# Mixture-of-experts stage on Trainium2: prompt rows picked by one-hot products ahead of the first expert, sample rows turned in pairs of blocks

## What is computed

```python
def ec_moe(h, w_router, w_gate, w_up, w_down):
    xf = h.reshape(N, D)
    aff = jax.nn.softmax((xf @ w_router).astype(jnp.float32), axis=-1)
    cap = CAPACITY_FACTOR * N // N_EXPERTS
    gates, idx = lax.top_k(aff.T, cap)
    xe = xf[idx]
    hid = jax.nn.silu(jnp.einsum('ecd,edf->ecf', xe, w_gate)) * jnp.einsum('ecd,edf->ecf', xe, w_up)
    ye = jnp.einsum('ecf,efd->ecd', hid, w_down) * gates[..., None].astype(h.dtype)
    out = jnp.zeros((N, D), h.dtype).at[idx.reshape(-1)].add(ye.reshape(-1, D))
```

## Time and profile before

| | us |
|---|---|
| median of 3 runs | 3549.77 (3549.66 to 3550.65) |
| the profiled execution's own time | 3553.03 |
| its span | 3551.3 |
| mean granted TensorE clock over the span | 0.968 |
| PE busy | 3315.4 (93%), 23082 matmuls |
| DVE busy | 2314.5 (65%) |
| ACT busy | 1628.7 (46%) |
| POOL busy | 638.6 (18%) |
| mean DMA rate | 153 GB/s |

### The profile page before, as it was taken

The page is one execution under the profiler, slowest core; times in us unless marked ns, Lnnn a source line. Parts: engine busy times, 40 slices in busy tenths (PEclk is TensorE's granted clock), DMA queues, the critical chain, the costliest instruction groups (busy, mean ns, idle before and its releaser), DMA issues. The chain is left out here.

```text
span 3551.3 us, 68456 instructions
## 1 busy us (share of the span) xinstructions
PE 3315.4 (93%) x23082; PEld 3024.3 (85%) x23082; DVE 2314.5 (65%) x3871; ACT 1628.7 (46%) x3584; POOL 638.6 (18%) x866
## 2 busy tenths in 40 slices
PE   7978999999999999999997992999999999999997
PEld 3877998998998998996665882999999999999997
DVE  3877887887887887886774446555555555555553
ACT  2435665665665665664442111433434334444332
POOL 0542222222222223221000000010100100000001
PEclk8999999999999999999998995999999999999998
DMA  6644434434434434433225542555666565555553
GB/s 222 219 178 140 128 114 153 127 114 153 127 114 153 127 114 134 129 114 105 95 67 208 194 183 83 178 176 178 181 187 188 185 185 179 179 178 178 179 179 85
DMA packets 357239, 542.43 MB, mean 153 GB/s; under 512 B 26104, under 2 KB 280568, under 8 KB 341882
## 3 DMA queue, kind: packets, MB, share of 16 engines
q1 hardware_dynamic: 346880, 505.26, 43.3%
q0 software_dynamic: 10240, 35.66, 4.6%
HBM read 439.11 MB, written 101.74 MB: 152 GB/s over the span
## 5 line engine op out<-in xcount | busy, mean ns | idle before, releaser
L2140 PE MATMUL ps_gu<-xT,e_w 128*128 128x272 f32 x6144 | 789.3, 290 | 5.8 <-DVE xT L2287 5.6
L2140 PEld LDWEIGHTS ps_gu<-xT,e_w 128*128 128x128 f32 x6144 | 779.6, 189 | 9.6 <-issue 9.3
L2282 DVE TENSOR_TENSOR e_w<-e_raw,e_w 128x2048 fp32r<-128x2048 f32 x192 | 440.0, 2292 | 341.8 <-ACT e_w L2207 325.5
L913 ACT ACTIVATE e<-ps_s,negm 128x1024 f32<-128x1024 f32 (+1 forms) x384 | 465.9, 1218 | 229.0 <-DVE negm L1195 229.0
L1187 DVE TENSOR_REDUCE mx<-ps_s 128x1 f32<-128x1024 f32 (+2 forms) x396 | 519.7, 1319 | 78.3 <-PE ps_s L642 78.3
L642 PE MATMUL ps_s<-kT,qT 128*128 128x512 f32 (+1 forms) x1920 | 473.8, 387 | 28.3 <-ACT e L913 16.8
L678 PE MATMUL ps_m<-v,aT 128*128 128x128 f32 x3456 | 477.2, 280 | 2.9
L678 PEld LDWEIGHTS ps_m<-v,aT 128*128 128x128 f32 x3456 | 424.1, 192 | 31.9 <-issue 16.1
L642 PEld LDWEIGHTS ps_s<-kT,qT 128*128 128x128 f32 x1920 | 351.8, 193 | 95.2 <-ACT e L913 16.5
L2159 PE MATMUL ps_gu<-hid,e_w 128*128 128x272 f32 x3072 | 417.6, 292 | 0.0
L712 PE MATMUL ps_m<-w,hT 128*128 128x384 f32 x2040 | 393.1, 341 | 3.4 <-DVE o L1242 1.8
(11 more groups left out here) (261 smaller groups left out, 3530.0 us busy)
## 6 DMA issues: line engine op xcount, KB each, us to landing
hT<-hT_d SPq DMA_DIRECT2D x85, 1024.0 KB, 5.6
e_raw<-w_gate SPq DMA_DIRECT2D x64, 1024.0 KB, 5.2
e_raw<-w_up SPq DMA_DIRECT2D x64, 1024.0 KB, 5.3
e_raw<-w_down SPq DMA_DIRECT2D x64, 1024.0 KB, 7.4
qT_d<-qT_out SPq DMA_DIRECT2D x96, 256.0 KB, 5.7
qT<-qT_d SPq DMA_DIRECT2D x96, 256.0 KB, 2.8
tab<-tabs_d SPq DMA_DIRECT2D x85, 256.0 KB, 2.7
hT_d<-hT SPq DMA_DIRECT2D x17, 1024.0 KB, 4.0
```

Source lines behind the costliest of these rows:

```text
L913: nc.scalar.activation(out, src, ACT.Exp, bias=negm[:, s.par, c:c + 1], scale=HD ** -0.5, accum_out=acc).then_inc(exp_done.sem, 1)
L2140: mm = nc.tensor.matmul(ps_gu[:, 2 * (s % 2) + f, 0:SLOTS], w_view(s, a)[:, k, f * P:f * P + P], xT[:, b, k, :], start=(k == 0 and a + b = ...
L2282: nc.vector.tensor_tensor(w[:, s % RING, 1, :], raw[:, s % RAW, :], w[:, s % RING, 0, :].bitcast(F32), ALU.subtract).then_inc(w_lo, 1)
```

## The change

The 16 prompt rows no longer go through the gather and the turns. The prompt's 128 rows of h2 are loaded once (`h2p`), a one-hot table of all 16 experts is made (`hot_all`), and 8 products of 256 columns (`pick`) yield the turned prompt rows of all experts, which ACT and DVE split into `xTp`. For each expert ACT then copies 256 elements per partition from `xTp` into `xT` (`place_prompt`). The sample rows are turned in four steps of four transposes, one step for each down slab. In a down slab the step and `turn_back(e, d - 1)` now both stand between the two halves. The diff, where lines are left out for length they are names, semaphores and the unchanged one-hot of expert e:

```diff
@@ -1994,7 +1994,11 @@
         g_cur = sb("g_cur", [P, 3])
         i_next = sb("i_next", [P, 3], U32)
         i_cur = sb("i_cur", [P, 3], U32)
-        xg = sb("xg", [P, 3, D])
+        xg = sb("xg", [P, 2, D])
+        h2p = sb("h2_prompt", [P, D])
+        hot_all = sb("hot_all", [P, NE, CAPP])
+        xTp = sb("xT_prompt", [P, NE, 2, KD, CAPP], F32R)
         xT = sb("xT", [P, 2, KD, SLOTS], F32R)
         sg_ = sb("silu_g", [P, 2, SLOTS])
         h32 = sb("e_h32", [P, 2, SLOTS])
...
-            return ps_gu[:, k % 4, :] if isinstance(e, int) and e == 0 else ps_x[:]
+        PAIRS = KD // 2
+        def turned_at(e, p):
+            bank = ps_gu[:, p, :] if isinstance(e, int) and e == 0 else ps_x[:]
+            return bank.rearrange("p (k c) -> p k c", k=2)
+        def picked_at(p):
+            return ps_d[:, p % 3, :].rearrange("p (k e c) -> p k e c", k=2, e=NE)
         def run_experts(eng, body):
...
@@ -2038,6 +2050,7 @@
         @block.sync
         def _(sp):
+            sp.dma_start(h2p[:], g.h2[NS * P:NT * P, :]).then_inc(h2p_in, 16)
             sp.dma_start(gate2[:, 0, :], g.mod[0, 5 * D:6 * D].partition_broadcast(P)).then_inc(gate2_in, 16)
             sp.dma_start(gate2[:, 1, :], g.mod[1, 5 * D:6 * D].partition_broadcast(P)).then_inc(gate2_in, 16)
@@ -2064,11 +2077,10 @@
             def gather(e):
                 hold(idx_done, e + 1)
-                hold(xT_ready, KD * e)
-                for n in range(3):
-                    rows = CAPP if n == 0 else P
-                    nc.gpsimd.indirect_dma_start(xg[0:rows, n, :], None, g.h2,
-                                                 bass.IndirectOffsetOnAxis(i_next[0:rows, n:n + 1], 0)
+                hold(xT_ready, PAIRS * e)
+                for n in range(2):
+                    nc.gpsimd.indirect_dma_start(xg[:, n, :], None, g.h2,
+                                                 bass.IndirectOffsetOnAxis(i_next[:, n + 1:n + 2], 0)
                                                  ).then_inc(gathered, 16)
             def scatter(e):
@@ -2095,24 +2107,37 @@
         def _(pe):
             def make_list(e):
                 wait_positive(pe, hot_done, 3 * e + 3)
-                wait_positive(pe, xT_lo, KD * e)
+                wait_positive(pe, xT_lo, PAIRS * e)
                 for half in range(2):
                     for t in range(NS):
                         nc.tensor.matmul(ps_x[:, 5 + 5 * half:10 + 5 * half], hot[:, t, half * P:half * P + P],
                                          vcur[:, t, :], start=(t == 0), stop=(t == NS - 1))
                 nc.tensor.matmul(ps_x[0:CAPP, 0:5], hot_p[:], vcur[:, NS, :], start=True, stop=True).then_inc(listed, 1)
-            def turn(e, k):
-                if k == 0:
-                    wait_positive(pe, gathered, 48 * e + 48)
+            def pick(p):
+                if p == 0:
+                    pe.wait_ge(h2p_in, 16)
+                    pe.wait_ge(hot_all_done, 1)
+                if p >= 3:
+                    pe.wait_ge(xTp_lo, p - 2)
+                for m in range(2):
+                    at = (2 * p + m) * P
+                    mm = nc.tensor.matmul(picked_at(p)[:, m], h2p[:, at:at + P], hot_all[:], start=True, stop=True)
+                mm.then_inc(xTp_ready, 1)
+            def turn(e, p):
+                if p == 0:
+                    wait_positive(pe, gathered, 32 * e + 32)
                     wait_positive(pe, found_done, 2 * e + 2)
-                bank = turned_at(e, k)
-                wait_positive(pe, xT_lo, k - 3 if isinstance(e, int) and e == 0 else KD * e + k)
-                for n in range(2):
-                    nc.tensor.transpose(bank[:, CAPP + n * P:CAPP + n * P + P], xg[:, 1 + n, k * P:k * P + P],
-                                        g.ident[:])
-                nc.tensor.transpose(bank[:, 0:CAPP], xg[0:CAPP, 0, k * P:k * P + P], g.ident[0:CAPP, 0:CAPP]
-                                    ).then_inc(xT_ready, 1)
+                bank = turned_at(e, p)
+                wait_positive(pe, xT_lo, 0 if isinstance(e, int) and e == 0 else PAIRS * e + p)
+                for m in range(2):
+                    at = (2 * p + m) * P
+                    for n in range(2):
+                        mm = nc.tensor.transpose(bank[:, m, n * P:n * P + P], xg[:, n, at:at + P], g.ident[:])
+                mm.then_inc(xT_ready, 1)
             def turn_back(e, d):
@@ -2130,7 +2155,8 @@
                     wait_positive(pe, w_lo, SLABS * e + s + 1)
                     q = s // 2
                     if s == 0:
-                        wait_positive(pe, xT_lo, KD * e + KD)
+                        wait_positive(pe, xT_lo, PAIRS * e + PAIRS)
+                        wait_positive(pe, xT_placed, e + 1)
                     if s < 2:
                         wait_positive(pe, yT_copied, 8 * e - 2 + 2 * s if before else 0)
                     wait_positive(pe, (silu_done, h32_done)[s % 2], 4 * e + q)
@@ -2170,18 +2196,21 @@
                         rest = range(6, KD)
                     else:
                         rest = range(KD)
-                    for f in range(2):
-                        down(f, rest)
-                        if more:
-                            turn(e + 1, 2 * d + f)
+                    down(0, rest)
+                    if more:
+                        turn(e + 1, d)
                     if d:
                         turn_back(e, d - 1)
+                    down(1, rest)
                 if not more:
                     turn_back(e, 3)
             make_list(0)
-            for k in range(KD):
-                turn(0, k)
+            for p in range(PAIRS):
+                pick(p)
+            for p in range(PAIRS):
+                turn(0, p)
+            pe.wait_ge(xTp_lo, PAIRS)
             run_experts(pe, body)
         def wait_read(eng, e, s):
...
-            def turned(e, k):
-                wait_positive(act, xT_ready, KD * e + k + 1)
-                nc.scalar.copy(xT[:, 0, k, :], turned_at(e, k)[:, 0:SLOTS]).then_inc(xT_hi, 1)
+            def picked(p):
+                act.wait_ge(xTp_ready, p + 1)
+                nc.scalar.copy(xTp[:, :, 0, 2 * p:2 * p + 2, :].rearrange("p e k c -> p k e c"), picked_at(p)
+                               ).then_inc(xTp_hi, 1)
+            def place_prompt(e):
+                if isinstance(e, int) and e == 0:
+                    act.wait_ge(xTp_lo, PAIRS)
+                wait_positive(act, slab_done, 8 * e)
+                src = xTp[:, bass.ds(e, 1)].rearrange("p o a k c -> p (o a) k c")
+                nc.scalar.copy(xT[:, :, :, 0:CAPP], src).then_inc(xT_placed, 1)
+            def turned(e, p):
+                wait_positive(act, xT_ready, PAIRS * e + p + 1)
+                nc.scalar.copy(xT[:, 0, 2 * p:2 * p + 2, CAPP:], turned_at(e, p)).then_inc(xT_hi, 1)
             def body(e, before, more):
                 for s in range(SLABS):
@@ -2228,13 +2269,18 @@
                         for f in range(2):
                             wait_positive(act, yT_ready, 8 * e + 2 * d + f + 1)
                             nc.scalar.copy(yT[:, d % 2, f, :], ps_gu[:, 2 * (d % 2) + f, 0:SLOTS]).then_inc(yT_copied, 1)
-                            if more:
-                                turned(e + 1, 2 * d + f)
+                            if more and f == 0:
+                                turned(e + 1, d)
+                        if more and d == 0:
+                            place_prompt(e + 1)
             for s in range(2):
                 split(0, s, True)
-            for k in range(KD):
-                turned(0, k)
+            for p in range(PAIRS):
+                picked(p)
+            place_prompt(0)
+            for p in range(PAIRS):
+                turned(0, p)
             run_experts(act, body)
...
+                wait_positive(dve, gathered, 32 * e)
                 wait_positive(dve, moved, 2 * e)
                 nc.vector.scalar_tensor_tensor(i_next[:], found[:, :, 1], float(P), found[:, :, 0], ALU.mult,
                                                ALU.add).then_inc(idx_done, 1)
@@ -2282,10 +2328,15 @@
                 nc.vector.tensor_tensor(w[:, s % RING, 1, :], raw[:, s % RAW, :], w[:, s % RING, 0, :].bitcast(F32),
                                         ALU.subtract).then_inc(w_lo, 1)
-            def turned(e, k):
-                wait_positive(dve, xT_hi, KD * e + k + 1)
-                nc.vector.tensor_tensor(xT[:, 1, k, :], turned_at(e, k)[:, 0:SLOTS], xT[:, 0, k, :].bitcast(F32),
-                                        ALU.subtract).then_inc(xT_lo, 1)
+            def picked(p):
+                dve.wait_ge(xTp_hi, p + 1)
+                hi, lo = (xTp[:, :, a, 2 * p:2 * p + 2, :].rearrange("p e k c -> p k e c") for a in range(2))
+                nc.vector.tensor_tensor(lo, picked_at(p), hi.bitcast(F32), ALU.subtract).then_inc(xTp_lo, 1)
+            def turned(e, p):
+                wait_positive(dve, xT_hi, PAIRS * e + p + 1)
```

(22 more changed lines are left out.)

## The result

The changed kernel takes 3580.67 us (3577.51 to 3582.31, 4 runs) where the kernel before takes 3550.21 (3549.66 to 3555.73, 4 runs): ratio 1.0077, 95% interval 1.0064 to 1.0090. The forecast was 3579 us, in a range of 3548 to 3598, and slower with a chance of 0.8. The profiled execution took 3580.08 us, span 3578.4.

What follows compares the result with a forecast made beforehand. PE was taken as the bound, by what it issues plus what it waits for. Terms 0.3 + 27.3 + 1.4 + 0.5 = +29.5 us on the profiled 3553.03, carried to a median 3.26 below it, gave 3579 us, range 3548 to 3598.

Steps and rivals of the forecast that it cites:

- The price of a turn: On PE in the expert loop: a turn costs 0.59 us before and 0.46 as four transposes, 0.116 each.
- The new wait: In slab 11, PE waits 3.37 us at turn_back(e, 2) for y_done, for the 15 experts with a successor.
- Cancelling: Slabs 8 to 11: saved issue time and new wait cancel, 31.47 against 31.45 us, +0.3 us in all.
- The clock: Behind each of 15 waits in the loop PE's clock falls, costing 1.8 us in the mean, 27.3 us.
- longer than the 2.25 that sufficed: Reason for one fall per wait: 3.37 us of idling exceeds the 2.25 us before a fall at the heads.
- The start: Expert 0's first products come later through the last picks and the prompt load: +1.4 us, between -1.25 and +7.8.
- after 2229: Sign at expert 0: if its products start after 2229, the picks are dearer than taken.
- The end: Behind the last expert's products, ACT's last copy is no longer covered by turn_back: +0.5 us.
- The clock holds: Rival for the expert loop: the waits bring no fall of the clock, 3552 us; chance 0.12.
- The clock stays low for longer, as transposes stand around: Rival for the loop: transposes don't help restore the clock, every fall is long, 45 us, 3597 us; chance 0.10.
- The wait is covered: Rival for slab 11: y_done comes within 3.48 us of slab 10's end, so it is faster, 3502 us; chance 0.08.
- The prompt rows' copy turns out in the path: Rival for ACT's placing copy in slab 8: its cover is gone, +6 us or so; chance 0.02.

Runs made afterwards that it cites:

- e6: The kernel before without the 16-column prompt transpose for experts 1 to 15: 3526.02 us against 3555.99, ratio 0.9911.
- e1: The changed kernel with DVE making result(e, 0) ahead of the split of slab 13: 3500.49 us against 3552.73 for the kernel before.
- e2: The changed kernel with turn_back(e, d - 1) put back behind both halves of its down slab: 3505.31 us, ratio 0.986 to the kernel before.
- e3: The changed kernel with 24 spare products on PE in front of turn_back(e, 2): 3553.11 us against 3552.73 for the kernel before.
- e9: The changed kernel with 4 spare products in front of turn_back(e, 2): 3560.48 us against 3552.43 for the kernel before.
- e4: The kernel before with only turn_back(e, d - 1) moved between the two halves of a down slab: 3619.73 us, ratio 1.0185.
- e8: The changed kernel with 12 spare products in front of turn_back(e, 2): 3555.60 us against 3555.99 for the kernel before.
- e5: e1 with SP's loads ahead of expert 0 reordered: slabs 0 and 1, prompt's rows, slabs 2 and 3, gates; 3498.29 us against 3555.99 for the kernel before.

## Why the prediction was right

- **The price of a turn** held: 0.59 us before, 0.22 without the 16-column piece (e6), 0.11 to 0.12 for each transpose. Without the new wait an expert was to take 3.35 us less; in e1 it takes 3.53 less (81.63 - 78.10).
- **The new wait** was to be 3.37 us, reckoned from load to load, for 15 experts; it is 3.36 between loads and 3.12 between matmuls. e1 and e2 remove it from either side.
- **Cancelling**: 31.47 against 31.45 us by the prediction, that is +0.02 an expert; measured -0.20 (81.43 against 81.63). A turn with a `turn_back` takes 1.10 us (2303.57 to 2304.67 in e1), not 1.16, twice, and `turn_back` behind the wait 0.61 (2809.97 to 2810.58), not 0.70.
- **The clock** was to fall behind all 15 waits for 1.8 us each, 27.3 us. It fell behind 13, for 1.3 to 2.7 each, 23.7 us for the 12 in the 14 steps and about 25 for all; e3, which takes only the falls away, is 27.6 us below the changed kernel. The total was nearly right because two errors lean against each other: the count was high and the price in the mean low, 1.8 where it was 2.0. The weak step is the argument "longer than the 2.25 that sufficed": e9's 2.61 us and e4's 2.97 us were followed by a fall in only 6 and 4 of 15, though both are longer than 2.25. That 13 of 15 fell here is in part luck. With a wait shorter by half a microsecond the forecast would have failed by that step, as e9 shows: 8 us above the kernel before instead of 30.
- **The start** was to cost +1.4 us and cost +3.75 (+2.1 to +3.8 over the seven traces of that order), a term that was mis-sized. The prediction had slab 1's split end near 2217.6; in the changed kernel it ended at 2223.7 (2221.42 + 2.29), 21.4 us after the first load and not 17.7. 1.5 us for the prompt's rows in the queue was too little: the split of slab 1 started 5.1 us later after the first load (19.08 against 13.94). From that split's end to the first product it took 7.7 us, less than the 8.0 to 9.4 of the prediction's path, although each pick product cost four times its low end (last section): the picks are dearer, as its sign "after 2229" says, but they are not what made the start late, and 2.5 us of 2231.45 come from the later start of the stage. That slabs 2 and 3 share the DMA engines with slab 1 would explain it, but no run took that apart. The chain of work shows slab 1 as its longest piece there:

```profile
2205.03 14.44 DMA e_raw<-w_up
```
- **The end** was to cost 0.5 us. The last result starts 76.9 us behind expert 15's first product, where it was 76.2, and `turn_back(15, 3)` waited 0.48 for the copy of yT (below). What follows that result took 1.1 us less than before, so expert 15 as a whole got no longer: 99.4 us against 99.8.

```profile
3555.01 0.87 PE L2150 MATMUL ps_d<-ident,e_yT 128*128 128x128 f32 x6 [0.48 <-ACT e_yT L2271]
```

- **The sum.** Within the stage the terms add up to +24.6 us, not +29.5. The medians differ by 30.5 all the same: 24.6, 2.5 for the later start of the stage, 2.8 by which the profiled execution of before lay above its median, and 0.6 for that of the changed kernel. So the mechanism and its order of size are shown; that 3579 lies within 2 us of 3580.67 is luck.
- **Signs.** The wait came 15 times, 50.4 us in all on the loads and 46.9 on the matmuls (forecast 50), PE was busy for 387.5 of 400 us (383) at a clock of 0.98 (0.97), and an expert took 1.5 us longer in the mean (1.8).
- **Rivals.** "The clock holds" is what e3 and e8 look like, and what the changed kernel does after 2 of 15 waits. "The clock stays low for longer, as transposes stand around" is out as the rule: 8 of 13 falls were of the short kind. "The wait is covered" is what e1 made, and its 3502 us were e1's 3500. "The prompt rows' copy turns out in the path" is out: e1 makes that copy and has PE busy for 800.00 of 800 us.

## What to carry to other kernels

When a step is moved earlier on the bounding engine, follow each of its waits back to what releases it, in the releasing engine's queue order: the move of `turn_back` by half a slab turned 1.2 us of cover into 3.1 us of waiting, behind a split that needed nothing from it. A gain in issue time on the bounding engine and a new wait can cancel exactly and still leave a loss, since the idling has a price of its own in the clock; filling a wait with useless work is a cheap test for that. And where a partner idles anyway (DVE ahead of the split in e1), putting the result that is waited for first costs nothing and here was worth 80 us: it turned a change that lost 30 us into one that gains 52.

## What the runs showed of the hardware that was not expected

Waits of the same length at the same place are sometimes followed by a fall of the clock and sometimes not. By idle time: 1.6 us, 0 of 15 (e8); 2.61, 6 of 15 (e9); 2.97, 4 of 15 (e4); 3.12, 13 of 15 (the changed kernel). So the share doesn't rise evenly with the length; 4 of 15 at 2.97 us stands in a loop whose common step is 85.26 us, with long runs of experts that all behave alike, while the steps of the other loops differ. The order of falls is not random either. In the changed kernel the steps from the second to the seventh are 84.02, 82.99, 84.13, 82.98, 82.69 and 81.43 us, and the next six repeat them to 0.06; in e9 every third wait from the third on is followed by a fall. That speaks for the moment at which a wait comes, besides its length. No run tested it, so what decides a single case stays open.

The pick products, 8 in the program, appear as 16 matmuls in the trace. In e1, where the first twelve run at a granted clock of 0.50:

```profile
2207.02 4.76 PEld L2126 LDWEIGHTS ps_d<-hot_all,h_prompt 128*128 128x128 f32 x12
```

Their loads start 0.43 us apart there, and 0.22 apart in e5 at a clock of 1.00. So one product of 256 columns with both operands in plain f32 costs 0.85 us at 1.2 GHz, four times the 0.21 that the prediction took as its low end at that clock, and 0.43 at 2.4 GHz. Six of the eight lay in idle time, so that it hardly showed.
